# Expert weights of a routed decoder layer: fetched by SyncE with plain DMAs instead of GpSimd's indirect ones

## What is computed

```python
def swiglu(x, wg, wu, wd):
    return (jax.nn.silu(x @ wg) * (x @ wu)) @ wd
# x: rows of 1024; wg, wu: (1024, 256); wd: (256, 1024), for each of 64 experts
# routed = sum over a token's 8 experts of gate * swiglu(x2[token], w_gate[e], w_up[e], w_down[e])
```

## Time and profile before

| | |
|---|---|
| median of 3 runs | 1554.72 us (1554.16 to 1556.8) |
| profiled execution, span | 1552.5 us |
| PE (TensorE) busy | 1490.0 us, 96% |
| DVE (VectorE) busy | 649.1 us, 42% |
| ACT (ScalarE) busy | 357.6 us, 23% |
| POOL (GpSimd) busy | 508.2 us, 33% |
| mean DMA rate | 282 GB/s, 437.30 MB |
| mean granted TensorE clock | 0.979 of full speed |

### The profile page before, as it was taken

How to read it: one execution, slowest core, us unless ns; L and a number is a source line. 1 busy time by engine, 2 the same in 40 slices (tenths; PEclk the granted TensorE clock), 3 DMA queues, 4 the chain that set the end, 5 groups by cost and what they waited for, 6 DMA issues and landing times.

```text
span 1552.5 us, 21508 instructions
## 1 busy us (share of the span) xinstructions
PE 1490.0 (96%) x8198; PEld 815.3 (53%) x8198; DVE 649.1 (42%) x1125; ACT 357.6 (23%) x674; POOL 508.2 (33%) x588
## 2 busy tenths in 40 slices
PE   4999999999999989999999999999999999999998
PEld 3444456777788758778645553333333333333333
DVE  4899982333231467437657821111111111111127
ACT  4111133322353323341224111111111111111120
POOL 2221100111000013100000256666666676666610
PEclk9999999999899899899999999999999999999999
DMA  9798645787512568728511499999999999999896
GB/s 343 277 323 291 248 134 200 261 296 263 185 50 81 183 193 283 257 87 299 173 54 55 191 362 418 416 417 419 392 389 397 353 421 417 417 348 386 352 359 278
DMA packets 138582, 437.30 MB, mean 282 GB/s; under 512 B 31526, under 2 KB 59546, under 8 KB 103678
## 3 DMA queue, kind: packets, MB, share of 16 engines
q0 software_dynamic: 65088, 303.29, 50.2%
q1 hardware_dynamic: 68080, 122.39, 22.9%
q10 hardware_dynamic: 5344, 10.65, 1.8%
HBM read 507.52 MB, written 45.61 MB: 356 GB/s over the span
## 4 chain that ended last, share of the span: by engine, by line
PE 84%; DMA 6%; DVE 3%; issue 3%; POOL 2%; ACT 2%; POOLq 0%; SPq 0%; another core or an unknown queue 0%; ACTq 0%; DVEq 0%
PE bank L2523 18%; PE bank L2137 15%; PE bank L2048 12%; PE bank L2548 9%; PE bank L2368 4%; PE bank L2356 4%; DMA arena<-in_w_exp_up_dram,arena 3%; PE bank L2509 3%; PE bank L2170 2%; PE bank L2595 2%; POOL arena L760 2%; PE bank L2394 1%; PE bank L2155 1%; PE bank L2295 1%; PE bank L2533 1%
## 5 line engine op out<-in xcount | busy, mean ns | idle before, releaser
L2523 PE MATMUL bank<-arena 128*64 128x512 f32 x1536 | 344.1, 599 | 7.5 <-DMA arena<-in_w_exp_up_dram,arena 5.8
L2137 PE MATMUL bank<-arena 128*128 128x260 f32 x1024 | 242.9, 393 | 0.0
L2523 PEld LDWEIGHTS bank<-arena 128*64 128x64 f32 x1536 | 105.9, 135 | 209.6 <-issue 204.4
L2137 PEld LDWEIGHTS bank<-arena 128*128 128x128 f32 x1024 | 195.7, 195 | 35.5 <-ACT arena L997 2.7
L2048 PE MATMUL bank<-arena 128*128 128x512 f32 (+1 forms) x448 | 189.8, 579 | 0.0
L2548 PE MATMUL bank<-arena 128*64 128x512 f32 x768 | 175.5, 598 | 0.5 <-ACT arena L1231 0.5
L1901 DVE TENSOR_TENSOR arena<-arena,bank 128x256 f32<-128x256 f32 x48 | 20.3, 423 | 358.4 <-issue 186.9
L2048 PEld LDWEIGHTS bank<-arena 128*128 128x128 f32 x448 | 83.5, 189 | 97.7 <-issue 90.3
L760 POOL DMA_INDIRECT arena<-in_w_exp_gate_dram,arena x96 | 98.1, 1022 | 100.0 <-issue 65.9
L760 POOL DMA_INDIRECT arena<-in_w_exp_up_dram,arena x96 | 96.1, 1001 | 30.7 <-issue 30.7
L760 POOL DMA_INDIRECT arena<-in_w_exp_down_dram,arena x96 | 95.2, 992 | 31.8 <-issue 30.0
(11 more groups left out here) (471 smaller groups left out, 1835.7 us busy)
## 6 DMA issues: line engine op xcount, KB each, us to landing
arena<-in_w_ada_dram SPq DMA_DIRECT2D x24, 1024.0 KB, 7.4
arena<-in_w_merge_gate_dram SPq DMA_DIRECT2D x16, 1024.0 KB, 6.7
arena<-expert_rows SPq DMA_DIRECT2D x16, 1024.0 KB, 13.5
arena<-in_w_in_dram SPq DMA_DIRECT2D x6, 2048.0 KB, 14.5
gate_logits<-arena ACTq DMA_DIRECT2D x32, 260.0 KB, 6.1
arena<-gate_logits SPq DMA_DIRECT2D x8, 1040.0 KB, 6.2
arena<-in_cache_swa_k_dram SPq DMA_DIRECT2D x24, 192.0 KB, 5.9
arena<-in_cache_swa_v_dram SPq DMA_DIRECT2D x24, 192.0 KB, 3.3
```

The lines of the kernel that those rows point to most:

```text
L2137: last = mm(o[:, 0:HALF], gate_place(q)[:, c, ms], hT[:, c, row_half[u % 2]], start=(c == 0), stop=(c == KC - 1))
L2523: ins = mm(bank[gu_bank[q]][r, :].rearrange("p (g n) -> p g n", g=2), xT[q][:, c, r], wgu[2 * q + lane][:, :, c, :], start=(c == 0), stop= ...
```

## The change

SyncE issues all loads of expert weights. VectorE writes a second, small table on one partition, `expert_p`: the expert's number for each cell (block and lane), 128 where the lane keeps its expert. SyncE loads a cell into a register (`value_load`), and issues plain DMAs whose source address is worked out from it and which are switched off (`cond`) where the number is not below 64; the semaphore counts in both cases. GpSimd keeps gathers and scatters, and copies only the four columns 2 to 5. The stores of the shared rows, SyncE's work before, are now threaded between the weight loads. The waits ahead of each load are those of before.

```diff
+        expert_p = view(TAB + 298, [LANES * MAXP], 1, dt=I32)
@@ SyncE
-            for t in range(TILES):
+            def shared_store(t):
                 sp.wait_ge(sem["sh_row"], t + 1)
                 load(shared[t * P:t * P + rows(t), :], sh[t][0:rows(t), :], sh_stored[t])
+            def expert_load(dst, tensor, cell, s):
+                e = sp.value_load(expert_p[:, bass.ds(cell, 1)], min_val=0, max_val=MISS // P)
+                for m in tensor:
+                    sp.dma_start(dst[m].unsqueeze(1), w_expert[m][bass.ds(e % NE, 1)].rearrange("e p n -> p e n"), cond=e < NE).then_inc(sem[s], 16)
+            def gate_up_load(p, q):
+                sp.wait_ge(sem["gu_done"], p * 3 + (q - 3))
+                sp.sem_inc(sem["x_col"], 1)
+                gate_up_lanes(p * 6 + (2 * q - 2), block_at(p, q, -1)[1])
+            def down_load(p, q):
+                sp.wait_ge(sem["dn_done"], p * 3 + (q - 4))
+                sp.sem_inc(sem["x_col"], 1)
+                down_lanes(p * 6 + (2 * q - 4), block_at(p, q, -2)[1])
+            shared_store(0)
             sp.wait_ge(sem["r_ready"], 1)
             last = sp.value_load(last_p, min_val=LAST_MIN - 1, max_val=MAXP - 2) + 1
+            gate_up_lanes(0, 0)
+            down_lanes(0, 0)
+            shared_store(1)
+            sp.wait_ge(sem["x1_out"], 16 * (TILES + 2))
+            gate_up_lanes(2, 1, range(1))
+            sp.wait_ge(sem["sh_gu"], TILES)
+            gate_up_lanes(2, 1, range(1, 2))
+            down_lanes(2, 1, range(1))
+            sp.wait_ge(sem["r_ready"], 2)
+            down_lanes(4, 2, range(1, 2))
+            shared_store(2)
+            sp.wait_ge(sem["sh_out0"], 32)
+            sp.wait_ge(sem["sh_out1"], 16)
+            gate_up_lanes(4, 2, range(1))
+            shared_store(3)
...
+            with sp.Fori(2, last + 1) as p:
+                for q in range(3):
+                    gate_up_load(p, q)
+                    down_load(p, q)
+            gate_up_load(last + 1, 0)
+            down_load(last + 1, 0)
+            down_load(last + 1, 1)
             sp.wait_ge(sem["r_ready"], 3)
@@ GpSimd
             def rest_order(p, q, end=0):
                 if end < 3:
                     pool.wait_ge(sem["x_t"], i - 2)
-                pool.wait_ge(sem["dn_done"], i - 4)
...
             def steady(p):
                 for q in range(3):
-                    gate_up_order(p, q)
-                    load_gate_up(block_at(p, q, -1)[1], order[q])
                     rest_order(p, q)
                     block_gather(q, order[q])
-                    load_down(block_at(p, q, -2)[1], order[q])
                     block_scatter(result_ready(p, q), order[q])
@@ VectorE
             lanes = bank[7][:, 0:LANES * MAXP].rearrange("p (s n) -> p s n", n=2)
+            ts_(expert_p, bank[7][0:1, 0:LANES * MAXP], 1.0 / P, float(MISS // P), ALU.mult, ALU.add)
```

More of the change, by code:

```diff
@@ L598, in _ @@
                 load(x1d[t * P:t * P + rows(t), :], xr[0:rows(t), t, :], "x1_out")
-            for t in range(TILES):
+            def shared_store(t):
                 sp.wait_ge(sem["sh_row"], t + 1)
                 load(shared[t * P:t * P + rows(t), :], sh[t][0:rows(t), :], sh_stored[t])
+            w_expert = [A[name][0].rearrange("e (p c) n -> e p (c n)", p=P) for name in ("w_exp_gate", "w_exp_up", "w_exp_down")]
+            def expert_load(dst, tensor, cell, s):
+                e = sp.value_load(expert_p[:, bass.ds(cell, 1)], min_val=0, max_val=MISS // P)
+                for m in tensor:
+                    sp.dma_start(dst[m].unsqueeze(1), w_expert[m][bass.ds(e % NE, 1)].rearrange("e p n -> p e n"), cond=e < NE).then_inc(sem[s], 16)
@@ new lines, in gate_up_lanes, with down_lanes @@
+            def gate_up_lanes(cell, b, lanes=range(2)):
+                for lane in lanes:
+                    expert_load([wgu[2 * b + lane][:, m, :, :].rearrange("p c n -> p (c n)") for m in range(2)], (0, 1), cell + lane, f"wg{b}")
+            def down_lanes(cell, b, lanes=range(2)):
+                for lane in lanes:
+                    expert_load([None, None, wdn[2 * b + lane].rearrange("p c n -> p (c n)")], (2,), cell + lane, f"wd{b}")
+            def gate_up_load(p, q):
+                sp.wait_ge(sem["gu_done"], p * 3 + (q - 3))
+                sp.sem_inc(sem["x_col"], 1)
+                gate_up_lanes(p * 6 + (2 * q - 2), block_at(p, q, -1)[1])
@@ new lines, in _ @@
+            gate_up_lanes(2, 1, range(1))
[9 more added lines that the diff above has]
+            shared_store(3)
+            sp.wait_ge(sem["sh_y"], TILES)
+            down_lanes(2, 1, range(1, 2))
@@ L607, in _ @@
+            gate_up_lanes(4, 2, range(1, 2))
+            down_lanes(4, 2, range(1))
+            shared_store(4)
+            gate_up_load(1, 1)
+            gate_up_load(1, 2)
+            down_load(1, 2)
+            with sp.Fori(2, last + 1) as p:
[5 more added lines that the diff above has]
+            down_load(last + 1, 1)
             sp.wait_ge(sem["r_ready"], 3)
@@ L755, in _ @@
                 step(pool.memset(xg[q], 0.0))
[L757 to L771, removed]
             def block_gather(q, at):
@@ L779, in block_scatter @@
                                         in_offset=None, bounds_check=TOK * TOPK - 1, oob_is_err=False).then_inc(sem[f"yst{q}"], 16)
[L781 to L790, removed]
             def rest_order(p, q, end=0):
@@ L800, in rest_order @@
                     pool.wait_ge(sem[f"yst{qb}"], pb * 16)
-                order_part(p, q, 2, 6)
-                pool.wait_ge(sem["pool_chain"], p * 6 + (n0 + 2 * q + 2 - end))
+                pool.sem_inc(sem["x_col"], 1)
+                pool.tensor_copy(order[q][:, 2:6], orders.rearrange("p s n -> p (s n)")[:, bass.ds(p * 18 + (6 * q + 2), 4)]).then_inc(sem["pool_chain"], 1)
+                pool.wait_ge(sem["pool_chain"], p * 3 + (n0 + q + 1))
                 pool.sem_inc(sem["x_col"], 1)
@@ L814, in _ @@
             last = pool.value_load(last_p, min_val=LAST_MIN - 1, max_val=MAXP - 2) + 1
[L815 to L821, removed]
             pool.wait_ge(sem["r_ready"], 2)
@@ L826, in _ @@
                 block_gather(q, row[q])
[L827 to L847, removed]
+            for q in range(3):
+                pool.wait_ge(sem["x_t"], q + 1)
+                block_gather(q, row[3 + q])
+            n0 = step.n - 6
             pool.wait_ge(sem["y_a"], 1)
@@ L865, in _ @@
                 p, q = block_at(last, k, 3)
-                if k == 0:
-                    gate_up_order(p, q)
-                    load_gate_up(block_at(p, q, -1)[1], order[q])
                 rest_order(p, q, end=k)
-                if k < 2:
-                    load_down(block_at(p, q, -2)[1], order[q])
                 block_scatter(result_ready(p, q), order[q])
```

## The result

| | before | changed |
|---|---|---|
| median of 4 runs each, us | 1555.53 (1554.16 to 1556.8) | 1567.8 (1565.65 to 1568.95) |
| span of the profiled execution, us | 1552.5 | 1567.2 |

The ratio is 1.0084, with a 95% interval of 1.0065 to 1.0103: the change makes the kernel 12 to 13 us slower. The forecast was 1558.1, its range ended at 1567. The sign was forecast, the size was not. In the code of the changed kernel the gate/up matmuls are L2525, the gather matmuls L2511, the down matmuls L2550, the final sum's products L2597 and L2614; SyncE's weight loads are L612, its register loads L610, its other loads L420; GpSimd's gathers are L818 and its scatters L822.

What follows compares the result with a forecast made beforehand. In the expert stage TensorE sets the beat, 12.13 us a block, and late weights are limited by bytes moved. Terms -0.8 + 3.4 + 0.3 + 0.5 = +3.4 us on 1554.72 gave 1558.1 us, range 1546 to 1567.

Steps and rivals of the forecast that it cites:

- What bounds the kernel: Expert stage: TensorE's beat of 12.13 us a block, late weights limited by bytes moved; at most 11.8 us to win.
- bytes: Expert weight loads: the same experts' weights move, nothing saved or added, 0 us.
- SyncE's budget: SyncE's added work in the expert loop: 3.4 to 9.6 us in a period of 12.13, so it keeps up; 0 us.
- Two queues: Expert stage: gathers and scatters on their own queue overtake weights of blocks 6, 13, 15; cost 3.4 us, bounds 0 and 5.
- Rival (b): Expert stage: gathers do not overtake weights, so the 3.4 us fall away: 1554.7 us; chance 0.08.
- rival (c): Expert stage: two queues cost 3% of bandwidth, 5.6 us: 1563.7, or 1566.2 with the tail's bound; chance 0.12.
- the first gather landing in 3 to 6 us: Start of the expert stage: sign that the forecast is right, the first row gather being served ahead of queued weights.
- Earlier issue: Start of the expert stage, from 898 us: weights issued sooner on SyncE; gain 0.8 us, bounds 0 and 4.7.
- VectorE, +0.3 us: Tables ahead of the first release: one more VectorE instruction delays TensorE by 0.3 us, bounds 0 and 0.4.
- The end: Final sum: expert-row fetches 6.5 us later behind the last conditional down loads, mostly covered; +0.5 us, bounds 0 and 3.
- a VectorE wait before its early row sums: Near the end: sign that the term for the delayed expert-row fetches, +0.5 us, is too small.

Runs made afterwards that it cites:

- b_pool_stores: The kernel before, its five shared-row stores threaded into GpSimd's weight loads where the changed kernel has them in SyncE's: 1560.84 us, ratio 1.0037.
- a_tail: The changed kernel, the first four expert-row fetches put ahead of the last conditional down loads: 1560.34 us, ratio 1.0027 to the kernel before.
- a_act: a_tail with the five shared-row stores issued by ScalarE on its own queue: 1556.48 us, ratio 1.0015 to the kernel before.
- b_tail: The kernel before, SyncE's first four expert-row fetches made to wait for the down product of the block before the last pass: 1557.01 us, ratio 1.0011.
- a_late: a_act with GpSimd's gathers and scatters one block later in the steady loop: 1555.36 us, ratio 1.0003 to the kernel before.

## Why the prediction was right or wrong

**What bounds the kernel, bytes, SyncE's budget.** Right. The beat stayed, the queue sizes came out as forecast. In the loop, SyncE's register load took 0.268 us and its issue 0.333 to 0.369 (medians), with 0.16 and 0.23 us for the register arithmetic; switched off, an issue took 0.073. The cell says 128 for that, not 64 as the prediction had it, which changes nothing. Its waits for TensorE in the loop sum to 214.0 and 60.2 us.

**Two queues, +3.4 us.** Right in mechanism: four row transfers of two kinds pass block 13's weights, 1.7 MB instead of 1.42. Two sub-steps were off: the first gather needed 9.4 us (904.56 to 913.97) and not 3 to 6, and the hardware queue moved 420 GB/s against 417, which over the 131 us up to block 13 gives 0.9 us back. Rival (b), no overtaking, falls by the count; rival (c), lost bandwidth, by the 419 to 421 GB/s (its 3% was also not half of what the row showed, (418 - 385) / 418 = 8%). The prediction's sign for this term, the first gather landing in 3 to 6 us, was missed.

**Earlier issue, -0.8 us (0 to 4.7).** The sign was wrong, and zero was a bound without a reason. The prediction saw that the stores move into the weight stream and noted only that the last one lands no earlier. It did not price the stores and their waits as work that now splits the weight stream: on GpSimd (b_pool_stores) that costs 5.8 us, and to take them out of a_tail gives 1.9 to 3.9, not resolved. With the stores elsewhere the gain that was forecast is there: a_act moves 0.8 MB more than before up to 946 us, 1.9 us.

**VectorE, +0.3 us.** Small and about right: from the instruction ahead of the one in the earlier trace rows to the long product behind the tables, 0.86 us (869.26 to 870.12) became 1.06 (871.67 to 872.73).

**All of it together before the end**: forecast +2.9, and a_tail, which has the end put right, is at 0.0027 or 4.2 us (1.9 to 6.5). The number fits, in part by luck: the passing took 1.7 MB and not 1.42, and the term beside it had the wrong sign.

**The end, +0.5 us (0 to 3).** This is the step that failed: the delay of the first four row fetches behind SyncE's last conditional loads. It cost 8.9 us by the ratios of changed kernel and a_tail, and 5.71 + 2.8 = 8.5 us in the trace. Four things in it:
- The delay was 8.7 us and not 6.5. From the end of the down product to the first fetch it took 4.2 us, where the prediction counted 2: two conditional lanes, the wait, and two register loads with bounds.
- The DMA work pushed back was 8.6 us (3.6 MB) and not about 5. The prediction looked at the earlier trace rows's one stretch at 1478 us; the changed kernel's engines ran nearly dry for three such stretches in a row (134, 0 and 68 GB/s, above).
- The cover was named but not measured. Against 5 us of work, a cost of 0.5 took 4.5 us of cover for granted; b_tail measures 3.5.
- The lower clock behind the wait added 2.8 us. It was counted behind each long wait in the earlier trace rows and put at nothing here.

With 8.5 us in place of this term's 0.5 the sum would have been 1566.1; its upper bound of 3 us left no room for that. The bounds of the whole forecast, 1555.5 to 1561, were also narrower than its terms' own, which add up to 1550 to 1563.1. The prediction named the sign of this failure (a VectorE wait before its early row sums), and it was there, with TensorE's 5.71 us behind it:

```profile
1523.63 2.61 DVE L1948 SCALAR_TENSOR_TENSOR arena<-arena 128x1024 f32<-128x1024 f32 x2 [3.77 <-DMA arena<-expert_rows]
```

**The late start.** 2.4 us of the profiled execution's 5.9 us at block 15 are no effect of the change: VectorE reaches the instruction ahead of the tables at 871.67 instead of 869.26. 32 matmuls some 100 us before the expert stage, which the change does not touch, took 16.18 us instead of 14.03; the granted clock from 766 to 772 us was 0.50, where it was 1.00 in the profile before. b_tail, whose program is the same up to 1474 us, has 16.21 us there and reaches its tables 1.7 us late, so this is a difference between executions; rates of fixed stretches are to be compared with it in mind.

```profile
767.69 14.03 PE L2368 MATMUL bank<-arena 128*128 128x512 f32 x32
```

```profile
767.89 16.18 PE L2370 MATMUL bank<-arena 128*128 128x512 f32 x32
```

**What is left.** With two causes undone and the third in part (a_late: 82.4 MB, where it was 81.3 before), the move of the weights from GpSimd to SyncE is worth nothing that these runs can tell (1.0003), though GpSimd's busy time fell from 508.2 to 212.6 us. That agrees with the rule of the Trainium skill's page "DMA: Bandwidth & Descriptors", section "Issuing engines are not separate DMA queues", that another issuer saves only sequencer time. Not tried: the changed kernel's weights with rows on the same queue, which would remove the overtaking alone.

## What to carry to other kernels

When work is moved to another engine's program, price everything it is now threaded between, in both directions: the fetches that now stand behind its last wait, and the stores that now split it. For a delayed transfer, measure the delay against the engine that wants the data, sum the work pushed back and the free DMA bytes until it is wanted, both in MB, and take the difference as the wait; add what the lower clock behind a wait of several microseconds costs. Here transfers on a queue of their own went ahead of a backlog, and the stream that was late by bytes got later by the bytes that passed (1.7 MB, 4.1 us); start such side transfers no earlier than they are needed.

## What the runs showed of the hardware

- A gather of some 0.36 MB on GpSimd's queue, beside some 12 MB queued on SyncE's (29 to 30 us at 420 GB/s, an estimate), lands after a median of 8.7 us (7.6 to 11.5, 16 gathers of the changed kernel); the weights need 29 to 30. The Trainium skill ("DMA: Bandwidth & Descriptors", "Queues, rings and completion order") has each engine take turns between its queues by packet; the passing agrees with it, but an equal share of 420 GB/s would land 0.36 MB in 1.7 us, an estimate from these rows, and the trace has five times that. What takes the rest was not found.
- In the full stretch from 946 us the core moves 420 GB/s with the weights as plain loads on the hardware queue (seven profiles) and 417 with them as indirect loads on the software queue (three profiles).
- After TensorE had waited 5.71 us at 1522 us, its next eight matmuls took 6.49 us instead of 3.71, at a granted clock of 0.66 from 1528 to 1536 us.
- A conditional load that is switched off costs SyncE 0.073 us of issue, against 0.333 to 0.369 (medians) for one that is on; its register work stays, 0.268 us for the load from SBUF and 0.16 and 0.23 us for the arithmetic.
